# Twelve and eight head tiles as seven half-size products per pair, in the query and key stage of the second model's two layers

## The reference, cut to what matters

```python
px = hx @ w_in
a_k, a_v, b_k, b_v, a_q, b_q, a_z, b_z, g_a, g_b = _split(px, SPLIT_SIZES)
pc = hc @ (w_in if update_ctx else w_in[:, :KV_COLS])
qa = _rmsnorm(hs(a_q, NA_HEADS), q_norm_a)
ka = _rmsnorm(hs(a_k, NA_HEADS), k_norm_a)
qb = _rope_2d(_rmsnorm(hs(b_q, GQA_Q_HEADS), q_norm_b), pos_row, pos_col)
kb = _rope_2d(_rmsnorm(hs(b_k, GQA_KV_HEADS), k_norm_b), pos_row, pos_col)
```

## Time and profile before

| what | us |
|---|---|
| median of 3 runs | 2858.41 (2855.77 to 2860.42) |
| the profiled execution | 2855.41 |
| its span, first to last instruction | 2853.7 |
| TensorE busy | 2780.5 (97%) |
| VectorE, ScalarE, GpSimd busy | 1235.1, 798.7, 598.2 |

### The profile page before, as it was taken

How to read it: one execution, slowest core, us unless ns; L and a number is a source line. 1 busy time by engine, 2 the same in 40 slices (tenths; PEclk the granted TensorE clock), 3 DMA queues, 4 the chain that set the end, 5 groups by cost and what they waited for, 6 DMA issues and landing times.

```text
span 2853.7 us, 44357 instructions
## 1 busy us (share of the span) xinstructions
PE 2780.5 (97%) x17684; PEld 1848.4 (65%) x17684; DVE 1235.1 (43%) x2313; ACT 798.7 (28%) x1595; POOL 598.2 (21%) x576
## 2 busy tenths in 40 slices
PE   5999999999999999999999999999999999999998
PEld 2777777777444446888544557775555554778887
DVE  3555555555122236777521125643223512553324
ACT  3344443433300002222101224651111122463210
POOL 0222221212000001555101101012223110103443
PEclk8999999999999999999999999999999999999999
DMA  5111011100424442444422211001111112101222
GB/s 213 58 35 42 31 42 35 42 24 24 168 68 162 140 147 93 166 169 175 153 83 75 78 44 45 1 1 59 59 60 58 59 67 77 45 2 45 89 74 89
DMA packets 61322, 221.21 MB, mean 78 GB/s; under 512 B 6688, under 2 KB 8864, under 8 KB 60896
## 3 DMA queue, kind: packets, MB, share of 16 engines
q1 hardware_dynamic: 42512, 153.11, 15.6%
q0 software_dynamic: 14656, 56.93, 5.9%
q10 hardware_dynamic: 3984, 8.71, 0.8%
HBM read 215.01 MB, written 2.15 MB: 76 GB/s over the span
## 4 chain that ended last, share of the span: by engine, by line
PE 95%; DVE 2%; DMA 1%; ACT 1%; issue 1%; ACTq 0%; POOL 0%; SPq 0%; DVEq 0%; POOLq 0%
PE psum L410 91%; PE psum L867 3%; DMA arena<-in_ctxT 1%; DVE arena L2090 0%; DMA arena<-in_stream 0%; DVE arena L2088 0%; PE psum L644 0%; DVE arena L1830 0%; DVE arena L1935 0%; DVE arena L1835 0%; ACT arena L1351 0%; ACT arena L1217 0%; DVE arena L2073 0%; PE psum L597 0%; DVE arena L1954 0%
## 5 line engine op out<-in xcount | busy, mean ns | idle before, releaser
L410 PE MATMUL psum<-arena 64*64 64x64 f32 (+7 forms) x16884 | 2685.9, 342 | 60.8 <-DMA arena<-in_ctxT 13.5
L410 PEld LDWEIGHTS psum<-arena 64*64 64x64 f32 (+4 forms) x16884 | 1761.6, 163 | 966.9 <-issue 616.6
L2254 POOL TENSOR_TENSOR arena<-arena 128x512 f32<-128x512 f32 (+1 forms) x68 | 83.7, 1231 | 618.3 <-DMA arena<-in_stream 311.4
L1705 DVE SCALAR_TENSOR_TENSOR arena<-arena 128x1024 f32<-128x1024 f32 x128 | 154.8, 1265 | 0.0
L1351 ACT ACTIVATE arena<-psum,arena 128x512 f32<-128x512 f32 (+2 forms) x160 | 115.3, 728 | 31.2 <-DVE arena L1946 17.4
L1908 DVE COPY arena<-psum 128x512 f32<-128x512 f32 x26 | 18.0, 692 | 220.9 <-PE psum L410 220.9
L1824 DVE TENSOR_TENSOR arena<-psum,arena 128x256 f32<-128x256 f32 (+1 forms) x68 | 31.7, 466 | 168.5 <-PE psum L410 168.5
L2225 POOL TENSOR_TENSOR arena<-arena 128x256 f32<-128x256 f32 x96 | 76.2, 810 | 132.5 <-PE psum L410 107.8
L2265 POOL TENSOR_TENSOR arena<-arena 128x512 f32<-128x512 f32 (+1 forms) x68 | 93.6, 1377 | 27.3 <-PE psum L410 27.0
L867 PE MATMUL psum<-arena 128*128 128x128 f32 x704 | 94.9, 280 | 4.2 <-ACT arena L1351 4.0
L867 PEld LDWEIGHTS psum<-arena 128*128 128x128 f32 x704 | 76.8, 141 | 29.3 <-ACT arena L1351 14.8
(11 more groups left out here) (251 smaller groups left out, 1761.7 us busy)
## 6 DMA issues: line engine op xcount, KB each, us to landing
arena<-in_stream SPq DMA_DIRECT2D x288, 512.0 KB, 3.3
arena<-in_mods POOLq DMA_DIRECT2D x80, 512.0 KB, 5.5
arena<-gc_rows POOLq DMA_DIRECT2D x16, 384.0 KB, 4.8
arena<-in_bias POOLq DMA_DIRECT2D x16, 384.0 KB, 3.8
arena<-in_xT ACTq DMA_DIRECT2D x1, 2048.0 KB, 17.5
out<-arena SPq DMA_DIRECT2D x1, 2048.0 KB, 7.2
arena<-in_conds ACTq DMA_DIRECT2D x1, 1536.0 KB
arena<-arena POOLq DMA_DIRECT2D x4, 384.0 KB, 4.3
```

Source lines behind the costliest of these rows:

```text
L410: return pe.matmul(out, lhsT, rhs, start=start, stop=stop, skip_group_check=True)
L1705: m = stt(mjunk[:, b % 2, :] if x < len(conds) - 1 else slot, slot, 0.5, cb[:, c, :], ALU.mult, ALU.mult, accum_out=dst(x))
L2254: add(sums[0], a21, a22, ALU.add).then_inc(s("wsum"), 1)
```

## The change

The pairs of tiles (0,1) to (10,11) in layer 0 and (4,5) to (10,11) in layer 1 are done with `seven_products`, six and four pairs. Layer 1's tiles 0 to 3 and tile 12 of both layers stay whole products. New places in the order:

- TensorE waits for all of `b2_va` before the first tile, in both layers. In a pair with first tile a, the head sum of a-2 and the last product of the pair before stand behind the first block product, and the head sum of a-1 behind the third (the new argument `second`). After the pairs: rotate(0), two blocks of tile 12, head sum 10, the last product, rotate(1), the other six blocks, head sum 11; rotate(2) and rotate(3) go into the value product `L_VB`.
- ScalarE does three snapshots a pair; Square and Ln/Exp (`head_square`, `head_root`) stand between them.
- VectorE's copies of paired tiles become three joins and one copy a pair; the scale of a-1 stands between `join_first` and `join_second`. All five rotations (`turn`) come after the pairs, and the one of tile 11 before the scale of tile 12.
- GpSimd forms the weight sums of each pair in a new buffer `WSq`. The two `VAs` transfers and the sums of two pairs go ahead of the bias tables; the negations go behind all pairs' sums.

```diff
-N_Z, N_MERGE, N_OUT2, N_LAYER = 0, 4, 20, 23
+N_Z, N_MERGE, N_OUT2, N_LAYER = 0, 4, 20, 29
+QK_PAIRS, QK_FIRST = (6, 4), (0, 4)
...
-    return N_UP + N_LAYER * l + stage
+    return N_UP + N_LAYER * l + QK_PAIRS[l] + stage
+
+
+def qk_at(l, p):
+
+    return pair_at(l, p - QK_PAIRS[l])
...
         hsq, hrn, rt1, rt2 = n2.take(2, TOK), n2.take(2, TOK), n2.take(SEQ), n2.take(SEQ)
+        WSq = n2.take(4, 4 * P)
+        assert n2.at <= rsum_at
...
-            def seven_products(n, banks, w1, w2, sums, kt, b, bt, input_sums, before=None, ready=None):
+            def seven_products(n, banks, w1, w2, sums, kt, b, bt, input_sums, before=None, ready=None, second=None):
                 part(z, sums[:, 0], bt[0], kt, True, False).then_inc(s("seven"), 1)
                 part(y, a12, b[1][0], kt, True, True, None if ready is None else (ready[0], ready[1] + kt))\
                     .then_inc(s("seven"), 1)
+                if second is not None:
+                    second()
                 pe.wait_ge(s("wsum"), 4 * n + 2)
                 pe.wait_ge(s("snap"), 3 * n + 1)
...
-                for n in range(13):
+                w = half_of(l)
+                Hq, HTl = quarters(H, 4, w), sums_of(HT2, 4, w)
+                banks = (0, 2, 3), (1, 2, 3)
+                pe.wait_ge(s("b2_va"), CH * l + CH)
+                if l == 0:
+                    pe.wait_ge(s("sq"), PRODUCTS[2] + 2 * KT)
+                    mm(psum[:, 6, :], ones, plain_sum).then_inc(s("nsum"), 1)
+                for n in range(QK_FIRST[l]):
                     pe.wait_ge(s("b2_raw"), 13 * l + max(n - 1, 0) + FREE)
-                    if n == 1:
-                        pe.wait_ge(s("b2_va"), CH * l + CH)
-                        if l == 0:
-                            pe.wait_ge(s("sq"), PRODUCTS[2] + 2 * KT)
-                            mm(psum[:, 6, :], ones, plain_sum).then_inc(s("nsum"), 1)
-                    product(T0 + L_QK + n, H, 2 * (n % 2), 2 * (n % 2) + 1 if wide or n in CTX_HEADS else None)
+                    product(T0 + L_QK + n, H, 2 * (n % 2), 2 * (n % 2) + 1)
                     if n:
                         head_sum(n - 1)
-                    if n >= 10:
-                        rotate(n - 10)
+                if l:
+                    pe.wait_ge(s("b2_raw"), 13 * l + 4 + FREE)
+
+                def ended(p):
+
+                    t = T0 + L_QK + QK_FIRST[l] + 2 * p + 1
+                    last_product(qk_at(l, p), banks[qk_at(l, p) % 2][0], weights(pe, t), 4, HTl, 2)
+
+                for p in range(QK_PAIRS[l]):
+                    n, a = qk_at(l, p), QK_FIRST[l] + 2 * p
+
+                    def before():
+
+                        head_sum(a - 2)
+                        ended(p - 1)
+
+                    if p >= 2:
+                        pe.wait_ge(s("b2_raw"), 13 * l + a - 2 + FREE)
+                    seven_products(n, banks[n % 2], weights(pe, T0 + L_QK + a), weights(pe, T0 + L_QK + a + 1), WSq, 4,
+                                   Hq, HTl, ("xsum", 4 * l + 4), before if p else None, None,
+                                   (lambda: head_sum(a - 1)) if a else None)
+
+                w12 = weights(pe, T0 + L_QK + 12)
+                pe.wait_ge(s("b2_raw"), 13 * l + 10 + FREE)
+                pe.wait_ge(s("join"), 3 * n + 2)
+
+                def last_head(ks):
+
+                    for k in ks:
+                        wk = w12[:, k * P:(k + 1) * P]
+                        mm(psum[:, banks[(n + 1) % 2][0], 0:SEQ], wk, H[:, k, 0:SEQ], k == 0, k == KT - 1)
+                        m = mm(psum[:, 3, 0:CTX], wk, H[:, k, SEQ:TOK], k == 0, k == KT - 1)
+                    return m
+
+                rotate(0)
+                last_head(range(2))
+                head_sum(10)
+                ended(QK_PAIRS[l] - 1)
+                rotate(1)
+                last_head(range(2, KT)).then_inc(s("used"), 1)
+                head_sum(11)
 
                 w = weights(pe, T0 + L_VB)
-                pe.wait_ge(s("b2_raw"), 13 * l + 12 + FREE)
                 for c in range(CH):
+                    if c == 2:
+                        rotate(2)
                     if c == 3:
                         head_sum(12)
+                    if c == 4:
                         rotate(3)
                     for k in range(KT):
...
-                for n in range(13):
-                    head_norm(l, n, KQ[:, n:n + 1, :] if n < 8 else bqk[n - 8])
+                def square(j):
+
+                    head_square(l, j, KQ[:, j:j + 1, :] if j < 12 else KB[:, None, :])
+
+                for n in range(QK_FIRST[l]):
+                    square(n)
+                    if n < QK_FIRST[l] - 1:
+                        head_root(l, n)
+                banks = (0, 2, 3), (1, 2, 3)
+                for p in range(QK_PAIRS[l]):
+                    n, a = qk_at(l, p), QK_FIRST[l] + 2 * p
+
+                    def first():
+
+                        head_root(l, a - 2)
+                        square(a - 1)
+
+                    snapshots(n, banks[n % 2], snaps2, half_of(l), True, first if p else None,
+                              (lambda: head_root(l, a - 1)) if a else None)
+                    square(a)
+                head_root(l, 10)
+                square(11)
+                head_root(l, 11)
+                square(12)
+                head_root(l, 12)
...
                 dve.wait_ge(s("b2_hex"), 13 * l + n + 1)
-                dve.wait_ge(s("b2_raw"), 13 * l + n + 1 + FREE)
+                if QK_FIRST[l] <= n < 12 and n % 2 == 0:
+                    dve.wait_ge(s("join"), 3 * qk_at(l, (n - QK_FIRST[l]) // 2) + 2)
+                else:
+                    dve.wait_ge(s("b2_raw"), 13 * l + n + 1 + FREE)
...
+                def ended(p):
+
+                    n, a = qk_at(l, p), QK_FIRST[l] + 2 * p
+                    dve.wait_ge(s("used"), T0 + L_QK + a + 2)
+                    dve.tensor_copy(KQ[:, a + 1, 0:w], psum[:, banks[n % 2][0], 0:w]).then_inc(s("b2_raw"), 2)
+
+                for n in range(QK_FIRST[l]):
+                    head_raw(l, n, blocks[n], 2 * (n % 2), 2 * (n % 2) + 1)
+                    if n:
+                        scale(n - 1)
+                for p in range(QK_PAIRS[l]):
+                    n, a = qk_at(l, p), QK_FIRST[l] + 2 * p
+                    x, y, z = banks[n % 2]
+                    if p:
+                        ended(p - 1)
+                        scale(a - 2)
+                    if l == 0 and p:
+                        for v in range(2 if p < 4 else 1):
+                            last_norm(2 * p - 2 + v if p < 4 else p + 2)
+                    join_first(n, y, snaps2, KQ[:, a, 0:w], w)
+                    if a:
+                        scale(a - 1)
+                    join_second(n, z, snaps2, KQ[:, a, w:2 * w], w)
+                    join_fourth(n, x, snaps2, KQ[:, a + 1, w:2 * w], w)
+                turn(0)
+                ended(QK_PAIRS[l] - 1)
+                scale(10)
+                turn(1)
+                head_raw(l, 12, blocks[12], banks[(n + 1) % 2][0], 3)
+                scale(11)
+                turn(2)
+                turn(3)
+                scale(12)
+                turn(4)
...
-                pool.wait_ge(s("b2_qk"), 13 * l + 1 + FREE)
-                load_tables(0)
-                load_tables(1)
-                negate_tables(0)
-                negate_tables(1)
+                def qk_sums(p):
+
+                    t = T0 + L_QK + QK_FIRST[l] + 2 * p
+                    weight_sums(qk_at(l, p), weights(pool, t), weights(pool, t + 1), 4, WSq)
+
                 pool.wait_ge(s("b2_va"), CH * l + XC)
                 pool.dma_start(VAs[0:HP], VAt[HP:P, 0:3, :]).then_inc(s("at_vs"), 16)
                 pool.dma_start(VAs[HP:P], VAt[0:HP, 1:4, :]).then_inc(s("at_vs"), 16)
+                qk_sums(0)
+                qk_sums(1)
+                pool.wait_ge(s("b2_qk"), 13 * l + 1 + FREE)
+                load_tables(0)
+                load_tables(1)
+                for n in range(2, QK_PAIRS[l]):
+                    qk_sums(n)
+                negate_tables(0)
+                negate_tables(1)
```

More of the change, by code:

```diff
@@ L1270, in _, with snapshots @@
             f(gl[:, 0, :], cf[:, 0, :], ACT.Gelu_apprx_tanh).then_inc(s("fg"), 1)
-            def snapshots(n, banks, snaps, w, after=True, ended=None):
+            def snapshots(n, banks, snaps, w, after=True, ended=None, second=None):
                 x, _, z = banks
@@ L1307, in _, with head_square, head_root @@
             norm_root(2, ((0, SEQ, 0),), eps=vec("eps", 5))
-            def head_norm(l, j, block_):
-                at = 0
+            def head_square(l, j, block_):
+                w = TOK if l == 0 or j in CTX_HEADS else SEQ
+                if QK_FIRST[l] <= j < 12 and j % 2 == 0:
+                    act.wait_ge(s("join"), 3 * qk_at(l, (j - QK_FIRST[l]) // 2) + 2)
+                else:
+                    act.wait_ge(s("b2_raw"), 13 * l + j + 1 + FREE)
```

(48 more changed lines are left out.)

9 lines of the change are left out of this document (3 added, 6 removed).

## The result

| | kernel before | changed kernel |
|---|---|---|
| median | 2856.14 us of 5 runs (2855.31 to 2860.42) | 2842.20 us of 5 runs (2837.94 to 2843.78) |
| profiled execution, its span | 2855.41, 2853.7 | 2837.94, 2836.2 |

The ratio of changed to before is 0.9947, 95% interval 0.9937 to 0.9958: 15.1 us faster, 12.0 to 18.0; the medians differ by 13.9. The forecast was 11.0 less, 2847.4. The direction is right, the gain is 3 to 4 us larger than forecast.

A forecast was written before the change was run, and what follows sets the result against it. TensorE, busy 97% of the span, was taken to bound the kernel. Columns -20.9, moved wait +6.5 and clock +3.4 gave -11.0 us, median 2858.41 to 2847.4; range 2841.5 to 2854.

The forecast's parts named there:

- Columns removed: Query and key pairs, both layers: an eighth of TensorE's columns goes, saving 14.8 and 6.1 us, together 20.9.
- the other bound: Head sum priced purely by columns, 1.29 and 0.86 us; the ten pairs then save 15.7 + 6.5 = 22.2 us.
- The moved wait: Ahead of the first tile, TensorE idles for the value copies, 3.25 us in each layer, 6.5 us in all.
- The clock behind that wait: Behind each new wait TensorE falls to half clock, 1.7 us a layer, 3.4 in all; bounds 0 and 3.4.
- Rival 1: The clock does not fall behind the new value-copy waits: -14.4 us, 2844.0, or 2842.7 with 22.2 for the columns; chance 0.18.
- What must hide: Inside the pairs, joins, snapshots, squares and roots cost nothing; closest slack 2 us in layer 0, 1.1 in layer 1.
- rival 3: In the pairs, head sum a-1 becomes a wait; with the root's 1.96 us bare in all ten, +8.6, 2867.0; chance 0.07.
- GpSimd: Weight sums and negations finish under cover of TensorE's pairs and cost nothing; without cover of the negations, up to 8 us.
- the lock: GpSimd's weight sums may block VectorE's scales in the pairs; taken as 0, bounds 0 and 0.5 us a pair, 5 us.
- the tail: Behind the pairs, tile 12's scale follows turn(3) and fits before rotate(4) by 0.3 us; 0, at worst 1 us a layer.
- Rival 2: Small waits in every pair from the lock or a late snapshot, 0.5 x 10: -6.0 us, 2852.4; chance 0.19.
- Rival 4: Fewer columns bring nothing because weight loading or issue bounds TensorE; only the waits are left, +9.9 us, 2868.3; chance 0.02.

The follow-up runs named there:

- e4: The kernel before with only the wait for all six value copies moved ahead of tile 0 in both layers; 2866.56 us, ratio 1.0035 to before.
- e2: Changed kernel plus 3.0 us of unused matmuls ahead of the value-copy wait in both layers; 2839.67 us beside 2841.87 for the changed kernel.
- e5: Changed kernel with the head sum of a-1 ahead of the second block product in eight pairs; 2858.22 us beside 2856.30 for the kernel before.
- e8: Changed kernel plus four unused 128x512 adds on GpSimd behind each pair's weight sums; median 2843.08 us.
- e6: Changed kernel with tiles 0 to 5 of layer 0 as whole products, three pairs left there; 2850.32 us, ratio 0.9981 to the kernel before.
- e7: Changed kernel with tiles 4 to 9 of layer 1 as whole products, one pair left there; 2849.18 us, ratio 0.9975 to the kernel before.
- e9: e3 with GpSimd's first-pair weight sums moved ahead of its value-copy wait and the two VAs transfers; 2834.31 us, ratio 0.9927 to the kernel before.
- e3: Changed kernel, value-copy wait put behind the first block product in layer 0, ahead of tile 1 in layer 1; 2835.77 us, ratio 0.9930 to before.

## Why the prediction came out as it did

- **Columns removed: right mechanism, 1.1 us too small.** Forecast 20.9 with 22.2 as the other bound; the stages gave 21.95 (15.54 and 6.41). Pair periods 20.69 and 13.83 where 20.8 and 13.9 stood. The small miss came from taking the product from one interval (10.28) and giving the head sum the rest, 1.36: the pairs give (20.69 - 18.09) / 2 = 1.30 for a wide head sum, near the 1.29 of the other bound.
- **The moved wait: right.** Two idle times of 3.18 us where 3.25 stood, at a price of 3.39 each, 6.8 us where 6.5 stood; e4 shows them in the kernel before by themselves, with nothing given back.
- **The clock behind that wait: the step that failed.** The step "I count 1.7 us in each layer" is right in size (1.72 by e2, 1.4 to 1.7 elsewhere) and nearly in frequency (13 of 16). Wrong was "three of three" as a law, and adding 3.4 us to a kernel that already held falls behind the attentions' starts, read in the earlier trace rows and left to stand as if they would come again. They come in some executions only. In the traces of the two kernels by themselves, before has two falls and one, 1.5 on average, the changed kernel one, two and two, 1.7: some 0.3 us more, an estimate from five traces, where 3.4 stood. In the two traces shown first one fall of 1.72 came and two of 1.57 and 1.53 went, so the clock's share of that difference was -1.38, not +3.4: with it, -21.95 + 6.78 - 1.38 - 0.29 (the lost wait in layer 0's attention) - 0.66 (the early part) gives the -17.50 of the spans. Without any difference in the clock and the early part it is -15.5, inside the 12.0 to 18.0 of the ratio. Rival 1's figure, -14.4, came nearer than the forecast, but partly by luck: its sentence, that the clock does not fall behind the new waits, holds for one of the six such waits in the changed kernel's three traces.
- **What must hide: right.** No idle time of TensorE in ten pairs. The slack is real and the place of the sum matters: e5 exposes 1.6 and 1.25 us a pair, 1.85 and 1.51 by the pace, which is rival 3 made by hand, and loses all of the gain. The rival's price of 1.96, for a bare root, is near that of the bare copy and square; its point of decision, 1.1 us a pair, rests on the 11.0 of the forecast and is 1.5 with the measured 15.1.
- **GpSimd, the lock, the tail: priced at nothing, and rightly.** Rival 2 is out by the trace of the changed kernel itself: no wait of TensorE inside a pair, though a scale took 1.97 us instead of 1.02 in layer 1 and one 2.46 in layer 0. e8 doubled GpSimd's work for 0.01 us; the scale of tile 8 was held up to 3.66 us under cover. What the Trainium skill's page "SBUF — State Buffer", section "SBUF: two separate sides", says of a held port pair agrees with the 2.46 and 3.66 us in kind. That the hold lasts for the whole instruction isn't shown: both scales end with the negation that they met, not a scale's length behind it, and one in layer 1 that started 0.6 us before a negation's end took its usual 0.74. That no one waits decides here. The tail's 0.3 us held: no idle time ahead of rotate(4), and the attention's starts keep their 1.96 and 2.02.
- **Rival 4: out.** e6 and e7 show each pair paying its eighth, 2.63 and 1.66 us.
- **The range.** Its low end was given as 2841.5, while its own terms, 2842.7 less one, make 2841.7.
- The Trainium skill ("TensorE: Matmul & The Clock Gate", section "Why this matters for your kernels") warns of gaps between bursts; the traces agree that they cost, and show that one and the same gap may or may not bring the clock down.

## What to carry to other kernels

When a stage is rebuilt, list the waits that end up in front of it: here one wait moved ahead by a single tile took back 6.8 of the 22 us that the pairs give, plus the clock, and could stand behind the first tile for nothing in layer 1 and behind the first block product for an idle time of 0.55 us in layer 0 (e9). A term that comes in some executions only (a fall of the clock) belongs into the forecast as a difference of two averages, and one profile gives such an average for neither kernel; stretches between fixed marks, net of it, compare to 0.1 us where medians spread by 5. A semaphore chain can be hidden or bare by its place alone: the same head sum costs no wait behind the third product and 1.85 us a pair ahead of the second (e5, layer 0).

## What the runs showed of the hardware that was not expected

- The same idle time of 3.18 us at the same instruction was followed by a half-rate clock in five traces and by a full one in three (layer 0). A fall lasts some 3.4 us and loses 1.7 us of work; it can begin while TensorE is still idle, and costs less then (1.5 to 1.6 us).
- A stop of TensorE cost 0.2 to 0.3 us more than the idle time in its bracket: 3.39 for 3.18 (e2 against e3), 1.85 and 1.51 for 1.59 and 1.25 (e5), 0.91 for 0.67 (e3 against e9).
- The first 1573 us of the program, the same in all these kernels, differ by up to 6.5 us between executions (1572.5 to 1579.0), about the spread of the single runs.
- A two-input VectorE operation of 1.02 us took 2.46 and 3.66 us beside GpSimd's negations, where the trace of the kernel before had shown 2.20. In all three cases it ended within 0.1 us of the end of the negation (4.08 us each): at 1612.36, 1685.04 and 1688.22 against 1612.42, 1685.11 and 1688.28. Spans on GpSimd are rough, so this is what the records show and no more.
